# A decoder trunk in split fp32 products: weight columns read as two halves in turns

## The reference

```python
z = h @ w_in                                   # layer 0: 2048 x 5120
return jnp.concatenate([a_out, b_out], axis=-1) @ w_out     # 2048 x 2048
...
q, k, v = jnp.split(h @ w_in, 3, axis=-1)      # layer 1: 2048 x 6144
return o @ w_out                               # 2048 x 2048
...
def squared_relu_mlp(h, w1, w2):               # both layers: 2048 x 8192, 8192 x 2048
    return jnp.square(jax.nn.relu(h @ w1)) @ w2
```

## Time and profile before

| | us |
|---|---|
| median of 3 runs | 2122.86 (2122.51 to 2123.09) |
| the profiled execution, whole | 2122.69 |
| its span, first to last instruction | 2120.7 |
| PE busy in it | 2111.2 |
| DVE busy | 1481.2 |
| ACT busy | 1028.1 |
| POOL busy | 20.1 |
| read from HBM | 403.41 MB, 191 GB/s over the span |

### The profile page before, as it was taken

How to read it: one execution, slowest core, us unless ns; L and a number is a source line. 1 busy time by engine, 2 the same in 40 slices (tenths; PEclk the granted TensorE clock), 3 DMA queues, 4 the chain that set the end, 5 groups by cost and what they waited for, 6 DMA issues and landing times.

```text
span 2120.7 us, 25442 instructions
## 1 busy us (share of the span) xinstructions
PE 2111.2 (100%) x9448; PEld 1748.5 (82%) x9448; DVE 1481.2 (70%) x1924; ACT 1028.1 (48%) x1180; POOL 20.1 (1%) x24
## 2 busy tenths in 40 slices
PE   9999999999999999999999999999999999999998
PEld 7888888888888888888888888888888888888886
DVE  6797867764774775586778778577746855764875
ACT  6444346543543453454645554665434544544553
POOL 0000001000000000000000000000000000000000
PEclk9999999999999999999999999999999999999999
DMA  9655555656656656655555555456556566656553
GB/s 323 207 179 171 191 193 170 206 195 187 195 199 190 186 198 218 184 193 198 178 179 178 179 178 199 160 160 216 199 186 192 180 213 182 198 197 214 183 199 119
DMA packets 204077, 406.81 MB, mean 192 GB/s; under 512 B 6544, under 2 KB 9936, under 8 KB 203472
## 3 DMA queue, kind: packets, MB, share of 16 engines
q1 hardware_dynamic: 203712, 405.37, 58.3%
q10 hardware_dynamic: 272, 0.16, 0.0%
HBM read 403.41 MB, written 2.10 MB: 191 GB/s over the span
## 4 chain that ended last, share of the span: by engine, by line
PE 99%; DVE 0%; DVEq 0%; ACT 0%; issue 0%; POOL 0%; POOLq 0%
PE ps L1203 99%; PE ps L1352 1%; DVE x_sb L767 0%; PE ps L1431 0%; DVE act_pair L1111 0%; DVE act_pair L773 0%; ACT tmp L497 0%; DVE y_sb L1081 0%; DVEq L110 0%; DVE w_lo L800 0%; PE ps L1257 0%; POOL rs_bc L350 0%; PE ps L1545 0%; PE ps L1550 0%; DVE rst L856 0%
## 5 line engine op out<-in xcount | busy, mean ns | idle before, releaser
L723 DVE TENSOR_TENSOR w_lo<-w_raw,w_hi 128x1024 fp32r<-128x1024 f32 x750 | 910.7, 1225 | 561.9 <-ACT w_hi L394 558.2
L394 ACT ACTIVATE w_hi<-w_raw 128x1024 fp32r<-128x1024 f32 x750 | 789.9, 1061 | 897.0 <-PE ps L1203 893.2
L1203 PE MATMUL ps<-w_hi,act_pair 128*128 128x512 f32 x3456 | 1072.0, 390 | 0.4 <-ACT w_hi L457 0.3
L1203 PEld LDWEIGHTS ps<-w_hi,act_pair 128*128 128x128 f32 x3456 | 647.1, 188 | 136.2 <-issue 2.0
L1203 PE MATMUL ps<-w_lo,act_pair 128*128 128x512 f32 x1728 | 670.2, 390 | 0.0
L1203 PE MATMUL ps<-w_hi,hid_hi 128*128 128x512 f32 x1280 | 498.7, 390 | 0.0
L1203 PE MATMUL ps<-w_hi,hid_lo 128*128 128x512 f32 x1280 | 498.0, 389 | 0.0
L1203 PE MATMUL ps<-w_lo,hid_hi 128*128 128x512 f32 x1280 | 498.0, 389 | 0.0
L1203 PEld LDWEIGHTS ps<-w_lo,act_pair 128*128 128x128 f32 x1728 | 324.1, 188 | 66.6 <-DVE w_lo L800 0.4
L829 DVE STREAM_TRANSPOSE qT<-kT 32x256 f32<-32x256 f32 x608 | 265.0, 436 | 42.2 <-ACT kT L605 32.8
L1203 PEld LDWEIGHTS ps<-w_hi,hid_lo 128*128 128x128 f32 x1280 | 240.2, 188 | 50.0
(11 more groups left out here) (104 smaller groups left out, 474.3 us busy)
## 6 DMA issues: line engine op xcount, KB each, us to landing
w_raw<-in_ffn_w_dram SPq DMA_DIRECT2D x256, 1024.0 KB, 5.3
w_raw<-in_sb_w_in_dram SPq DMA_DIRECT2D x48, 1024.0 KB, 5.1
w_raw<-in_ab_w_in_dram SPq DMA_DIRECT2D x36, 1024.0 KB, 5.2
w_raw<-in_ab_w_out_dram SPq DMA_DIRECT2D x16, 1024.0 KB, 5.0
w_raw<-in_sb_w_out_dram SPq DMA_DIRECT2D x16, 1024.0 KB, 5.0
w_raw<-in_ab_w_in_dram SPq DMA_DIRECT2D x6, 512.0 KB, 8.5
x_sb<-in_x_dram SPq DMA_DIRECT2D x8, 256.0 KB, 7.2
gpost<-in_norm_post_mix_dram SPq DMA_DIRECT2D x2, 1024.0 KB, 7.9
```

Of the source, the lines that this page charges most:

```text
L394: nc.scalar.activation(w_hi[:, t % RING, :, :], w_raw[:, t // 2, h:h + 2, :], ACT.Copy).then_inc(hi_ready, 1)
L723: nc.vector.tensor_tensor(w_lo[:, t % RING, :, :], w_raw[:, t // 2, h:h + 2, :], w_hi[:, t % RING, :, :].bitcast(F32), ALU.subtract).then_ ...
L1203: return nc.tensor.matmul(dst, lhsT, rhs, start=start, stop=stop, skip_group_check=True)
```

## The change

Every product of 512 weight columns reads them in another order: one column from the first half of the stored row (0 to 255), one from the second (256 to 511), and so on. So that PSUM gets its columns in the order it had, ACT and DVE store them for that: column 2c + h of the raw row goes to place c of half h. The conversions therefore read raw weights in steps of two and write in runs of 256. Sizes, the number of instructions, waits and queues stay as they were. Products of activations alone (scores, values, the sums with `soft_hi`) keep `mm`.

```diff
+        def by_parity(raw):
+
+            return raw.rearrange("p k (c h) -> p k h c", h=2)
+
+        def in_halves(w):
+            return w.rearrange("p k (h c) -> p k h c", h=2)
...
-                nc.scalar.activation(w_hi[:, t % RING, :, :], w_raw[:, t // 2, h:h + 2, :], ACT.Copy
+                nc.scalar.activation(in_halves(w_hi[:, t % RING, :, :]), by_parity(w_raw[:, t // 2, h:h + 2, :]), ACT.Copy
                                      ).then_inc(hi_ready, 1)
...
-                nc.vector.tensor_tensor(w_lo[:, t % RING, :, :], w_raw[:, t // 2, h:h + 2, :],
-                                        w_hi[:, t % RING, :, :].bitcast(F32), ALU.subtract).then_inc(lo_ready, 1)
+                nc.vector.tensor_tensor(in_halves(w_lo[:, t % RING, :, :]), by_parity(w_raw[:, t // 2, h:h + 2, :]),
+                                        in_halves(w_hi[:, t % RING, :, :].bitcast(F32)), ALU.subtract).then_inc(lo_ready, 1)
...
+            def halves(cols):
+
+                return cols.rearrange("p (h c) -> p c h", h=2)
+
+            def mm_w(dst, lhsT, w, start, stop):
+                return mm(dst, lhsT, halves(w), start, stop)
+
             def tick_tokens(buf, s, slot, hi, lo, ready, hi_done=(), opens=True):
...
-                            mm(dst, hi[:, kt, tok], w_hi[:, slot, i, :], opens and kt == 0, False)
-                        mm(dst, hi[:, kt, tok], w_lo[:, slot, i, :], False, False)
-                        last = mm(dst, lo[:, kt, tok], w_hi[:, slot, i, :], False, kt == KT - 1)
+                            mm_w(dst, hi[:, kt, tok], w_hi[:, slot, i, :], opens and kt == 0, False)
+                        mm_w(dst, hi[:, kt, tok], w_lo[:, slot, i, :], False, False)
+                        last = mm_w(dst, lo[:, kt, tok], w_hi[:, slot, i, :], False, kt == KT - 1)
```

More of the change, by code:

```diff
@@ L456, in first_kt @@
                     act.wait_ge(landed, 16)
-                    nc.scalar.activation(w_hi[:, kt // 2, kt % 2, :], w_raw[:, 0, kt, :], ACT.Copy).then_inc(done, 1)
+                    i = kt % 2
+                    nc.scalar.activation(in_halves(w_hi[:, kt // 2, i:i + 1, :]), by_parity(w_raw[:, 0, kt:kt + 1, :]), ACT.Copy
+                                         ).then_inc(done, 1)
                 first_kt(0, s_kt[0], s_kt_hi)
@@ L799, in first_kt @@
                     dve.wait_ge(converted, n)
-                    nc.vector.tensor_tensor(w_lo[:, kt // 2, kt % 2, :], w_raw[:, 0, kt, :],
-                                            w_hi[:, kt // 2, kt % 2, :].bitcast(F32), ALU.subtract).then_inc(done, 1)
+                    i = kt % 2
+                    nc.vector.tensor_tensor(in_halves(w_lo[:, kt // 2, i:i + 1, :]), by_parity(w_raw[:, 0, kt:kt + 1, :]),
+                                            in_halves(w_hi[:, kt // 2, i:i + 1, :].bitcast(F32)), ALU.subtract
+                                            ).then_inc(done, 1)
                 first_kt(0, s_kt_hi, 1, s_kt_lo)
@@ L1231, in closing_ticks @@
                             dst, tok, slot = ps[:, 2 * buf + b, :], slice(b * P, (b + 1) * P), s % RING
-                            mm(dst, hid_hi[:, kt, tok], w_hi[:, slot, i, :], False, False)
-                            mm(dst, hid_hi[:, kt, tok], w_lo[:, slot, i, :], False, False)
-                            last = mm(dst, hid_lo[:, kt, tok], w_hi[:, slot, i, :], False, kt == KT - 1)
+                            mm_w(dst, hid_hi[:, kt, tok], w_hi[:, slot, i, :], False, False)
+                            mm_w(dst, hid_hi[:, kt, tok], w_lo[:, slot, i, :], False, False)
+                            last = mm_w(dst, hid_lo[:, kt, tok], w_hi[:, slot, i, :], False, kt == KT - 1)
                         if b == 1:
@@ L1243, in products @@
                     for b in range(TB):
-                        last = mm(ps[:, b, :], act[:, 2 * s + i, b * P:(b + 1) * P], w[:, s, i, :],
+                        last = mm_w(ps[:, b, :], act[:, 2 * s + i, b * P:(b + 1) * P], w[:, s, i, :],
                                   s == 0 and i == 0 and act is act_hi and w is w_hi, False)
@@ L1307, in opening_ticks @@
                     for i in range(2):
-                        mm(ps[:, 2 * buf + 1, :], act_hi[:, 2 * s + i, P:T], w_hi[:, s, i, :], s == 0 and i == 0, False)
+                        mm_w(ps[:, 2 * buf + 1, :], act_hi[:, 2 * s + i, P:T], w_hi[:, s, i, :], s == 0 and i == 0, False)
                 pe.wait_ge(lo_ready, 8 * u + 1)
@@ L1311, in opening_ticks @@
                 for i in range(2):
-                    mm(ps[:, 2 * buf + 1, :], act_hi[:, i, P:T], w_lo[:, 0, i, :], False, False)
-                    last = mm(ps[:, 2 * buf + 1, :], act_lo[:, i, P:T], w_hi[:, 0, i, :], False, False)
+                    mm_w(ps[:, 2 * buf + 1, :], act_hi[:, i, P:T], w_lo[:, 0, i, :], False, False)
+                    last = mm_w(ps[:, 2 * buf + 1, :], act_lo[:, i, P:T], w_hi[:, 0, i, :], False, False)
                 last.then_inc(pe_ticks, 1)
@@ L1317, in opening_ticks @@
                     for b in range(TB):
-                        mm(ps[:, 2 * buf + b, :], act_hi[:, 2 + i, b * P:(b + 1) * P], w_lo[:, 1, i, :], False, False)
+                        mm_w(ps[:, 2 * buf + b, :], act_hi[:, 2 + i, b * P:(b + 1) * P], w_lo[:, 1, i, :], False, False)
                 late_transposes(k, 1)
@@ L1322, in opening_ticks @@
                     for b in range(TB):
-                        last = mm(ps[:, 2 * buf + b, :], act_lo[:, 2 + i, b * P:(b + 1) * P], w_hi[:, 1, i, :], False, False)
+                        last = mm_w(ps[:, 2 * buf + b, :], act_lo[:, 2 + i, b * P:(b + 1) * P], w_hi[:, 1, i, :], False, False)
                 last.then_inc(pe_ticks, 1)
@@ L1362, in block0_hi @@
                     for i in range(2):
-                        mm(ps[:, 0, :], act_hi[:, 2 * s + i, 0:P], w_hi[:, s, i, :], s == 0 and i == 0, False)
+                        mm_w(ps[:, 0, :], act_hi[:, 2 * s + i, 0:P], w_hi[:, s, i, :], s == 0 and i == 0, False)
                 pe.wait_ge(post_done, u - 1)
@@ L1396, in block0_lo @@
                 for i in range(2):
-                    mm(ps[:, 0, :], act[:, i, 0:P], w[:, 0, i, :], False, False)
+                    mm_w(ps[:, 0, :], act[:, i, 0:P], w[:, 0, i, :], False, False)
             def late_transposes(k, s):
```

## The result

The changed kernel takes 2085.85 us (median of 4 runs, 2084.78 to 2086.49) against 2122.82; the ratio is 0.9825, 95% interval 0.9808 to 0.9842. Faster by 37 us, inside the wide range and on the side forecast, but 60 us short of the 2026 us, and outside the forecast's own range of 2002 to 2063. That the wide range holds it is no merit: it lies where no case of the prediction had its time. The direction was right, and so was where the gain came from, the order in which products read; most of what was gained was given back, by slower conversions, which the prediction had only as a rival, with another cause and on DVE alone.

What follows compares the result with a forecast made beforehand. The prediction took PE's 9024 products of 512 columns, at 226.67 ns from start to start, to bound the kernel. It summed 2122.7 - 99.6 (read order) + 3 (DVE's lag) = 2026 us, range 2002 to 2128.

Steps and rivals of the forecast that it cites:

- the wide range: Whole time from 2002 us, past the case of no change, to 2128 us; given 0.81 chance.
- the forecast's own range: The faster case, chance 0.68: 2002 us with no loss left to 2063 us with half of it left.
- What bounds the kernel: PE, with no wait left to remove: 9024 products of 512 columns, 226.67 ns start to start, 96% of the time.
- (1), the read order: Products of 512 weight columns on PE reading halves in turns save 11.04 ns each, 99.6 us in all.
- the prediction's own sign: Mechanism wrong if a product's time moves and reading two adjacent runs in turns would move it as much.
- The rivals on TensorE: PE's products: order makes no difference, 2123 us, chance 0.14; or each jump costs, over 300 ns a product, chance 0.13.
- (3) and (4), the conversions: ACT's and DVE's stepped conversions: nothing taken; upper bounds +0.87 us on ACT and +1.08 us on DVE.
- The other sign of being wrong: Mechanism wrong if PE gains and idle time before L1203 takes it back; PE's waits should stay under 10 us.
- What cover was left: ACT's upper end, 651 us, fits its idle 1093 us; DVE's cover is thinner, so its upper end became a rival.
- the rival: DVE's conversions cost double, 1.08 us more each: 2293 us, deciding from some 0.8 us more; chance 0.05.
- What is late next: DVE falls behind PE in about ten dense stretches, at most 0.7 us each: 0 to 7 us, 3 taken.

Runs made afterwards that it cites:

- e5_near16: The change, but weights stored in blocks of 16 even then 16 odd columns, products reading the two runs in turns 64 bytes apart: 2036.46 us, ratio 0.9591.
- e1_order_only: The change, but both conversions read and write in runs as before; only the products read the halves in turns: 2031.77 us, ratio 0.957.

## Why the prediction was right and wrong

**What bounds the kernel** was right: no wait to remove, only 9024 starts.

**(1), the read order,** was right in size: 215.6 ns forecast, 216.1 in the change and 215.86 with the order alone, 97.5 us for 99.6. But no run shows what the 215.6 ns, and with it the 11.04 ns of the sum, was made of; it was the author's estimate, and so was the loss of which the range's ends leave none (2002 us) or half (2063). What the runs showed in its place is 226.67 ns for one run and 215.86 for halves in turns, and no order below 215.7. Nor is it enough that each place is asked for an element less often: four places in turns took 269 to 283 ns, and 0, 2, 1, 3 gained nothing (226.7). So the value was in part luck. By the prediction's own sign it was also wrong in mechanism: adjacent runs in turns move a product's time as much as far halves do (215.86 ns in e5_near16). Why two runs of four columns or more gain, and no other order tried does, stays open.

**The rivals on TensorE**, no difference and a cost of each jump, both fell to e1_order_only: same type, same instructions, another order, 10.8 ns less. The over 300 ns named for the second, and the times far above 2200 us that go with it, were an estimate that no run shows for halves in turns; it was other orders that took so long (halves by twos 340, eight runs of 16 440, a step of two 451).

**(3) and (4), the conversions,** are the step that failed. "I take nothing" was the measured answer for the stepped read beside the old products (1225 ns on DVE, 1130 on ACT), and wrong beside the new ones (1512, 1566). The bounds of +0.87 and +1.08 us held the values. What I did not ask is whether a changed access on one engine changes the price of another engine's access to the same memory. Each edit was priced as if made alone. No row of before could show the pair. The other sign of being wrong came true here: PE gained, and its waits, to stay under 10 us, came to 40.7 before L1214 and L1449.

**What cover was left** was the second fault. ACT's higher price was called covered because 651 us fit in 1093 idle ones; 505 ns more cost 24 us all the same, 16 of them in layer 1's attention, where PE waits for what ACT computes between its conversions. For DVE the rival took the average of a whole upward group, 62.94 of 87 us, and found that it decides from 0.8 us more. Less than that hurts: the units in a group differ, and a middle one has DVE busy for 17.7 of 21.8 us (its durations, 8 x 1.225 + 16 x 0.436 + 2 x 0.685, add up to 18.1). There 0.32 to 0.38 us more fills the 20.7 us, and 0.29 came, on top of DVE's waits for ACT.

**What is late next** was allowed 0 to 7 us; the order alone gave back 6.4, so the 3 taken was low.

In sum: 99.6 was 97.5; the 3 was 6.4; and 54 us were missing from the sum, 24 by ACT, 21 by DVE and 9 by both.

## What to carry to other kernels

When a change alters how an engine walks through memory, price the other engines' walks through the same memory again, together; and test both halves of a change apart, since here one alone gained 91 us, the other alone made no difference, and both together gained 37. Idle time is cover only in the stretch where the work is added: take the densest unit, not the average of its group. Where PE reads fp32r columns in one run, two near runs in turns are worth a try: 4.8% less a product here (215.86 for 226.67 ns), at no instruction.

## What the runs showed of the hardware that was not expected

- A product of 512 fp32r columns takes 226.7 ns read in one run and 215.7 to 216.0 ns read from two runs of 4 to 256 in turns; the other orders tried took 226.7 to 451 ns (the table above).
- A stepped read (every second f32) on ACT or DVE costs next to nothing by itself (1130 for 1061 ns, 1225 for 1225), but 1.5 to 1.6 us beside 216 ns products that read two runs in turns from places 256 bytes or more apart; at 128 bytes or less at most 1.17 and 1.23. "Halves in turns by fours" (1 KB, 250 ns) does it too (1539 and 1504). Quarters (512 bytes, 283 ns) and halves by twos (1 KB, 340 ns) do not (1141 and 1164, 1226 and 1228). So both a far distance and a fast product were there in each slow case; the two were not tried apart beyond this, and why 256 bytes stays open.
- Writing 1024 elements to two places 1 KB apart in turns takes 2.05 us on ACT and 2.12 on DVE, 1.9 and 1.7 times the 1.06 and 1.22 us of runs, whatever the products do.
- After 2.9 us of waits of PE in layer 1 (only ACT stepping) the granted clock was down, 0.50 from 1087.0 to 1090.0 us and 0.71 on average from 1088 to 1092, and the tick took 7.6 us. After the same wait elsewhere the clock stayed up (1.00 from 1232 to 1238), and the tick took 6.0. So such a wait cost 1.6 us more than its length, or nothing more.
